# Spreading the PEER gates: one fp32 product per token, or two rounded (fp32r) products with the gate in two parts

## The reference, cut to what matters

```python
ids = jnp.take_along_axis(cand_i, best_pos, axis=-1)      # i * 128 + j
g = jax.nn.softmax(best_s, axis=-1)
...
ub = jnp.take(u_tab, idb, axis=0)
act = jax.nn.gelu(jnp.einsum('tkd,td->tk', ub, xb))
vb = jnp.take(v_tab, idb, axis=0)
return jnp.einsum('tk,tkd->td', gb * act, vb)
```

## Time and profile before

| | us |
|---|---|
| runs timed (3) | 2165.93 median, 2165.83 to 2167.42 |
| the profiled execution | 2171.05 |
| its span in the profile | 2169.3 |
| PE busy in it | 2108.0 (97%) |
| the stretch of the spreads | about 690 to 807 of the span |

### The profile page before, as it was taken

The page is one execution under the profiler, slowest core; times in us unless marked ns, Lnnn a source line. Parts: engine busy times, 40 slices in busy tenths (PEclk is TensorE's granted clock), DMA queues, the critical chain, the costliest instruction groups (busy, mean ns, idle before and its releaser), DMA issues.

```text
span 2169.3 us, 31600 instructions
## 1 busy us (share of the span) xinstructions
PE 2108.0 (97%) x12416; PEld 1897.5 (87%) x12416; DVE 1376.8 (63%) x1874; ACT 704.3 (32%) x745; POOL 4.8 (0%) x11
## 2 busy tenths in 40 slices
PE   7999998998999998999999999999999999999997
PEld 5888887887988998999999999989999999999785
DVE  6675575568788986556565655655555565654675
ACT  2014112005311344434334343433434334342432
POOL 0000000000000000000000000000000000000000
PEclk8999999999999999999999999999999999999999
DMA  9999595994443458555555555655555565555552
GB/s 390 421 419 362 197 365 236 380 421 172 171 155 116 180 216 319 206 179 209 188 218 193 195 207 176 219 189 207 204 183 207 186 222 189 200 206 177 196 193 78
DMA packets 98649, 496.12 MB, mean 229 GB/s; under 512 B 8256, under 2 KB 41312, under 8 KB 43040
## 3 DMA queue, kind: packets, MB, share of 16 engines
q1 hardware_dynamic: 83280, 373.81, 45.9%
q10 hardware_dynamic: 14112, 115.35, 14.0%
q0 software_dynamic: 1200, 6.16, 0.7%
HBM read 473.14 MB, written 22.15 MB: 228 GB/s over the span
## 4 chain that ended last, share of the span: by engine, by line
PE 89%; DMA 7%; DVE 3%; ACT 1%; issue 0%; ACTq 0%; DVEq 0%; SPq 0%; POOL 0%
PE ps L470 19%; PE ps L459 11%; PE ps L460 11%; PE ps L461 11%; PE ps L725 5%; PE ps L727 5%; PE ps L726 5%; PE ps L714 5%; PE ps L715 5%; PE ps L716 5%; DMA mod_first<-wmod 4%; PE ps L671 3%; DMA mod_ring<-wmod 1%; DVE mod_first L1112 1%; DMA wraw<-wst 1%; DVE rstd L1088 0%
## 5 line engine op out<-in xcount | busy, mean ns | idle before, releaser
L461 PE MATMUL ps<-h_hi,wlo 128*128 128x256 f32 x1952 | 553.3, 283 | 0.0
L459 PE MATMUL ps<-h_hi,whi 128*128 128x256 f32 x1728 | 490.0, 284 | 5.4 <-ACT act_u L954 5.4
L460 PE MATMUL ps<-h_lo,whi 128*128 128x256 f32 x1728 | 490.0, 284 | 0.0
L1411 DVE TENSOR_TENSOR yacc<-yacc,ps 128x512 f32<-128x512 f32 x256 | 176.1, 688 | 404.5 <-PE ps L727 404.5
L461 PEld LDWEIGHTS ps<-h_hi,wlo 128*128 128x128 f32 x1952 | 375.5, 192 | 0.0
L1377 DVE TENSOR_TENSOR vlo<-vraw,vhi 128x2048 fp32r<-128x2048 f32 x116 | 260.8, 2289 | 135.3 <-ACT vhi L1001 135.3
L459 PEld LDWEIGHTS ps<-h_hi,whi 128*128 128x128 f32 x1728 | 332.7, 193 | 7.6 <-issue 5.6
L460 PEld LDWEIGHTS ps<-h_lo,whi 128*128 128x128 f32 x1728 | 332.7, 193 | 2.0
L470 PE MATMUL ps<-hid,wraw 128*128 128x256 f32 x1344 | 296.6, 381 | 4.7 <-DVE hid L1258 4.7
L470 PEld LDWEIGHTS ps<-hid,wraw 128*128 128x128 f32 x1344 | 256.6, 191 | 40.7 <-issue 4.9
L1373 DVE TENSOR_TENSOR wlo<-wraw,whi 128x2048 fp32r<-128x2048 f32 x120 | 269.4, 2285 | 16.6 <-ACT whi L977 16.6
(11 more groups left out here) (239 smaller groups left out, 2336.1 us busy)
## 6 DMA issues: line engine op xcount, KB each, us to landing
vraw<-vtab SPq DMA_DIRECT2D x116, 1024.0 KB, 6.7
wraw<-wst SPq DMA_DIRECT2D x108, 1024.0 KB, 4.8
wraw<-wst ACTq DMA_DIRECT2D x94, 1024.0 KB, 7.1
mod_ring<-wmod SPq DMA_DIRECT2D x74, 1024.0 KB, 12.6
mod_first<-wmod SPq DMA_DIRECT2D x22, 1024.0 KB, 20.0
gates_dram<-gstage ACTq DMA_DIRECT2D x4, 4096.0 KB, 16.8
gring<-gates_dram SPq DMA_DIRECT2D x64, 256.0 KB, 5.1
wraw<-vtab SPq DMA_DIRECT2D x12, 1024.0 KB, 5.0
```

Source lines behind the costliest of these rows:

```text
L459: mm(dst, hi, src_hi, start=first, stop=False)
L460: mm(dst, hi, src_lo, start=False, stop=False)
L461: return mm(dst, lo, src_hi, start=False, stop=last)
```

## The change

Each token's single fp32 product becomes two fp32r products that accumulate in the same PSUM bank: `hot_a`.T @ `hot_b` with the gate's rounded upper part, and `hot_a`.T @ `hot_lo` with the remainder. ACT writes the rounded gates `gate_hi` (one more copy out of PSUM per half of the tokens). DVE computes once, for all 256 tokens, `gate_part` = (gate - gate_hi) / max(gate_hi, 1e-30) in four instructions. ACT makes `hot_lo` for each token by multiplying DVE's `hot_b` by the token's `gate_part` (one number per partition). PE waits for `hot_lo` in place of `hot_b`. In ACT's stream the remainder's one-hots of spread m+3 stand ahead of the copy of spread m, after three sets made up front; its loop is written out.

```diff
-        hot_a = at("hot_a", 173.5, [HOT_RING, GT, P])
-        hot_b = at("hot_b", 181.5, [HOT_RING, GT, P])
+        hot_a = at("hot_a", 173.5, [HOT_RING, GT, P], F32R)
+        hot_b = at("hot_b", 181.5, [HOT_RING, GT, P], F32R)
+        hot_lo = at("hot_lo", 149.5, [HOT_RING, GT, P], F32R)
+        gate_hi = at("gate_hi", 217.5, [T], F32R)
+        gate_part = at("gate_part", 218.5, [T])
@@ PE, spread
-                pe.wait_ge(s_hot, n + 1)
+                pe.wait_ge(s_hotlo, n + 1)
...
                 for t in range(GT):
-                    r = mm(ps_spread[r_][:, t, :], hot_a[:, r_, t, :], hot_b[:, r_, t, :], start=True, stop=True)
+                    mm(ps_spread[r_][:, t, :], hot_a[:, r_, t, :], hot_b[:, r_, t, :], start=True, stop=False)
+                    r = mm(ps_spread[r_][:, t, :], hot_a[:, r_, t, :], hot_lo[:, r_, t, :], start=False, stop=True)
@@ ACT
                 A(picks[:, :, tt * P:(tt + 1) * P], ps_spread[tt][:, 0:3], ACT.Copy).then_inc(s_pkr, 1)
+                A(gate_hi[:, tt * P:(tt + 1) * P], ps_spread[tt][:, 2], ACT.Copy).then_inc(s_ghi, 1)
+
+            def one_hots_lo(r_, n, first=False):
+                act.wait_ge(s_hot, n + 1)
+                if not first:
+                    act.wait_ge(s_gmm, n - (HOT_RING - 1))
+                for t in range(GT):
+                    r = A(hot_lo[:, r_, t, :], hot_b[:, r_, t, :].bitcast(F32), ACT.Copy,
+                          scale=gate_part[:, bass.ds(n * GT + t, 1)])
+                r.then_inc(s_hotlo, 1)
...
+            act.wait_ge(s_part, 1)
+            for n in range(HOT_RING - 1):
+                one_hots_lo(n, n, True)
...
-                    with act.Fori(0, per // HOT_RING) as i:
-                        for r_ in range(HOT_RING):
-                            act.wait_ge(s_gmm, i * HOT_RING + (m0 + r_ + 1))
-                            A(gstage[...], ps_spread[r_].rearrange("p t b -> p b t"), ACT.Copy).then_inc(s_gev, 1)
+                    for m in range(m0, m0 + per):
+                        if m + HOT_RING - 1 < SPREADS:
+                            one_hots_lo((m + HOT_RING - 1) % HOT_RING, m + HOT_RING - 1, m == 0)
+                        act.wait_ge(s_gmm, m + 1)
+                        A(gstage[...], ps_spread[m % HOT_RING].rearrange("p t b -> p b t"), ACT.Copy).then_inc(s_gev, 1)
                     early_gelu(b)
@@ DVE
             dve.wait_ge(s_pkr, 2)
+            dve.wait_ge(s_ghi, 2)
+            own.did(V.tensor_scalar(ms[:, 0, :], gate_hi[:].bitcast(F32), 1e-30, None, ALU.max)); own.settle()
+            own.did(V.reciprocal(ms[:, 1, :], ms[:, 0, :]))
+            own.did(V.tensor_tensor(gate_part[:], picks[:, 2, :], gate_hi[:].bitcast(F32), ALU.subtract)); own.settle()
+            V.tensor_tensor(gate_part[:], gate_part[:], ms[:, 1, :], ALU.mult).then_inc(s_part, 1)
...
-                    b, g = (picks[:, i, bass.ds(n * GT + t, 1)] for i in (1, 2))
+                    b, g = picks[:, 1, bass.ds(n * GT + t, 1)], gate_hi[:, bass.ds(n * GT + t, 1)].bitcast(F32)
                     r = V.tensor_scalar(hot_b[:, r_, t, :], iota, b, g, ALU.is_equal, ALU.mult)
```

More of the change, by code:

```diff
@@ L314, in hybrid_block @@
                                           sem("picks_transposed"), sem("picks_read"))
+        s_ghi, s_part, s_hotlo = sem("gate_hi"), sem("gate_lo_over_hi"), sem("one_hots_lo")
         s_hot, s_gmm, s_gev = sem("one_hots"), sem("gates_spread"), sem("gates_staged")
@@ L985, in _ @@
                     m0 = (b - FIRST) * per
-                    with act.Fori(0, per // HOT_RING) as i:
-                        for r_ in range(HOT_RING):
-                            act.wait_ge(s_gmm, i * HOT_RING + (m0 + r_ + 1))
-                            A(gstage[:, q % 2, :, bass.ds((i * HOT_RING + (m0 - q * 2 * per + r_)) * GT, GT)],
-                              ps_spread[r_].rearrange("p t b -> p b t"), ACT.Copy).then_inc(s_gev, 1)
+                    for m in range(m0, m0 + per):
+                        if m + HOT_RING - 1 < SPREADS:
+                            one_hots_lo((m + HOT_RING - 1) % HOT_RING, m + HOT_RING - 1, m == 0)
+                        act.wait_ge(s_gmm, m + 1)
+                        A(gstage[:, q % 2, :, bass.ds((m - q * 2 * per) * GT, GT)],
+                          ps_spread[m % HOT_RING].rearrange("p t b -> p b t"), ACT.Copy).then_inc(s_gev, 1)
                     early_gelu(b)
```

## The result

| | median us | range | runs |
|---|---|---|---|
| before | 2167.29 | 2165.83 to 2168.65 | 8 |
| after | 2172.48 | 2171.83 to 2176.13 | 8 |

The ratio is 1.0027, 95% interval 1.0016 to 1.0038: the change makes the kernel 5.2 us slower (3.5 to 8.2), where +6.6 was forecast. The profiled execution of after took 2171.83 us with a span of 2170.0. It isn't slower by 5 us than the profiled one of before (2171.05, 2169.3), because the parts that the change does not touch happened to be quicker, 1.8 us ahead of the spreads and 0.9 us behind them. So I compare the stage itself, from the start of the second turning of the picks to the first product of block 20: 806.78 - 689.36 = 117.42 us before, 808.40 - 687.54 = 120.86 us after, +3.4 us.

A forecast was written before the change was run, and what follows sets the result against it. PE bounds the kernel (97% busy), DVE nearly a second bound in the stage. Products 0, start +4.4, clock +0.7, stop +1.5 give +6.6 us: 2177.7 profiled, 2172.5 timed, say 2173; range 2162 to 2184.

The forecast's parts named there:

- the likeliest case: Whole kernel: products cost nothing, start, clock and stop add +6.6 us, 2173 us timed; chance 0.52.
- two of its terms: More half clock after the longer first wait, +0.7 us, and ACT's stop after chunk 18, +1.5 us.
- Products: PE's spreads: two fp32r products per token cost what one fp32 product did, change 0, ends -23 and +57 us.
- The choice of 0.111 us by the weight load: PE's spread records: the load of 128 columns limits a short fp32r product, 0.111 us each as before.
- The straight line through the products of 256 and 512 columns: PE's spread records: fp32r pace carried down to 128 columns gives 0.066 us, the lower end.
- rival (1): Spreads: fast products, 0.066 us a record, another engine sets the pace; 2168 us by ACT, 2163 by DVE; chance 0.26.
- Start: Before PE's first spread: `gate_hi` copy 0.25, four DVE instructions 2.9, ACT's first remainder 1.27; +4.4 us.
- Clock: Start of the spreads: PE's longer wait adds a little more half clock, +0.7 us, bounds 0 and 2.5.
- The stop at the third store: After chunk 18: ACT waits for the store and makes `whi`, PE waits for spread 59's remainders; +1.5 us, bounds 0 and 4.
- Behind the stage: After the spreads: PE's stop moves as a whole and absorbs nothing; its 5.44 us wait stays.
- ACT: Steady steps: four remainders, copy out and chunk-end share need 1.69 of 1.76 us, so ACT just fits.

The follow-up runs named there:

- two experiments with half operands: Changed kernel with 64 moving columns in both fp32r products, 2271.45 us; changed kernel with a stationary operand of 64 columns, 2168.88 us.
- start-only kernel: Kernel before with the four DVE instructions ahead of the first one-hots, their results unused: 2171.12 us, ratio 1.0018.
- the one with the fp32 product: Changed kernel with one fp32 product per token, `hot_b` alone; ACT still makes `hot_lo` and PE waits for it: 2172.90 us, ratio 1.0024.
- the two kernels with shared work: Changed kernel without the remainder, ACT multiplying three of four tokens' gates: 2148.94 us; the same with ACT's stop and first `whi` four spreads later: 2144.91 us.
- the repeat: Changed kernel unchanged, because an edit's condition held in all 64 spreads: 2172.25 us, ratio 1.0021.
- split start: Changed kernel with `gate_part` made in three pieces, the first of 16 tokens, DVE starting on the first half of the picks: 2170.12 us, ratio 1.0012.
- `whi` twice: Changed kernel with ACT making the first `whi`, after chunk 18, twice: 2173.96 us, ratio 1.0029.
- the stationary operand of 64: Changed kernel with `hot_a`'s first 64 columns as stationary operand in both fp32r products, all 128 moving columns kept: 2168.88 us, ratio 1.0003.
- six-copy kernel: Changed kernel with the remainder's copies of two of a set's four tokens each cut into two of 64 columns: 2194.03 us, ratio 1.0120.
- upper part only: Changed kernel without `hot_lo`, `gate_part` and its four DVE instructions, one fp32r product per token: 2156.87 us, ratio 0.9954.
- later `whi`: Shared-work kernel (no remainder, ACT multiplying three tokens' gates) with ACT's stop and first `whi` four spreads later: 2144.91 us, ratio 0.9891.

## Why the prediction was right, step by step

The forecast was +6.6 us and 2173, the likeliest case; 2172.48 and +5.2 were measured. Direction, place and mechanism were right: the products cost nothing, the start costs 4.3 us. That the forecast of 2172.5 was met to 0.1 us is luck: it stood on a median of before of 2165.93 from three runs, which is 2167.29 over eight, and two of its terms, worth 2.2 us together, were not found.

- **Products: 0 forecast, 0 found.** The choice of 0.111 us by the weight load was right, and the two experiments with half operands show the reason given to be the right one. The straight line through the products of 256 and 512 columns is not wrong, but it holds only while the product covers its load: with the load halved, 128 columns do run at 0.06. With the whole load the records stay about 0.11 us apart at 64 columns as at 128, so the fast products of rival (1) did not come. The rule of the Trainium skill (TensorE: Matmul & The Clock Gate, LDWEIGHTS), columns over 1.2 GHz, 107 ns for 128, agrees with the 0.11 us at full clock; at the half clock the measured 0.213 us is twice that, so here the load follows the granted clock, where the rule has one number. That a load hides behind one product only, which the prediction says in the same sentence, does not stand in that section; the traces of this case bear it out, since the records behind the four long ones of the chunk steps are 0.11 apart from the second on, as if no load had been made ahead.
- **Start: +4.4 forecast, +4.3 found** (7.22 - 2.88). DVE's four took 2.74 us for 2.9, ACT's first set 1.28 for 1.27, and the wait for `gate_hi` made DVE begin 0.24 us later for 0.25.
- **Clock: +0.7 forecast, -0.9 found.** From the first spread to block 20 the stage took 113.6 us after and 114.5 before. The half clock ended 4.2 us behind the first spread (699.0) where it had taken 6 us before, so less work fell into it. In the start-only kernel it is -1.3 us and in the one with the fp32 product -0.4. All of these are differences to one execution of before, and this length varies from one execution to the next: in the two kernels with shared work, which are the same up to the end of chunk 18, the first spread comes 2.64 us behind the picks in both, and the third starts 5.08 us behind the first in one and 3.56 in the other. So the term of +0.7 was not found, and the sign of what is in its place is not shown.
- **The stop at the third store: +1.5 forecast, 0 found.** This is the step that failed. ACT reached the stop when I said (796.6, t + 1.5 for t + 1.4, t being the start of spread 56 at 795.1), but the store had landed: at most 14.2 us after its issue, where the forecast carried over the 16.3 us of before. So ACT did not wait the 2.4 us, and `whi` alone, 1.8 us, is covered by the three sets of lead. With `whi` doubled the wait of PE appears, 0.97 us, which shows the mechanism as right; what was wrong is the duration of the DMA. This was no chance of one execution: the third store was there within 13.9 to 14.3 us, without a wait, in the repeat and in the kernels with one fp32 product, split start, `whi` twice and the stationary operand of 64 too, while start only, with the spacing of before, has 16.2 us. Why it lands sooner no run tests. One thing that differs is that ACT issues the load of weights 1.8 us ahead of the store in place of 0.5.
- **Behind the stage: nothing absorbed.** The remainder of the span is 1361.6 us after and 1362.5 before, and PE's stop there ends 23.6 us behind the start of the last spread for 23.8. It follows the last spread, as forecast. The kernels whose block 20 began late show the other side of it: what PE loses between the last spread and the stop is taken back.
- **ACT: 1.69 us a step forecast, 1.65 and the chunk ends found**, and the six-copy kernel places the bound where it was put.

The sum from the trace is 4.3 - 0.9 + 0 = 3.4 us in the stage. The timed +5.2 (3.5 to 8.2), and the repeat's +4.6 (2.6 to 6.5), are a little more. The repeat's interval has the 3.4 in it, and the half clock at the start, which moves by 1.5 us between executions of the same code, is one candidate. Where this last 1 to 2 us lies isn't shown, and I leave it open.

## What to carry to other kernels

The short products here are paced by the load of their stationary operand: two one-pass products of 128 by 128 (0.11 us each) cost what one fp32 product does. Of what would help, the runs show fewer products (10 us gained) and a narrower stationary operand (0.06 us a record), and the rows of 256 columns show wider ones (0.12 us for twice the columns). Before giving a neighbour engine work to relieve PE, add up its instructions per step, and price what now stands in front of the first product; here that start was the whole loss that the traces show. And in a stage where several engines are within 0.1 us of each other, look at each one's single long stops: a wait of 2.40 us cost another 3 us through the clock. A duration of a DMA is a weak thing to carry over to a kernel that issues its transfers at other times: here 16.3 us became at most 14.2.

## What the runs showed of the hardware that I had not expected

- PE with every record back to back, products of 64 moving columns behind loads of 128 between fp32 chunk steps, stayed at 1.2 GHz for over 200 us after it had fallen there in a wait, and cost 99 us against the changed kernel. The same records, started at 2.4 GHz, kept it for the rest of the stage (57 us, one execution).
- The load of 128 columns follows the granted clock: 0.11 us at 1.00 and 0.213 at 0.50, with products of 128 or 64 columns. With a load of 64 columns, 128 moving columns are 0.06 and 0.107 us apart.
- Waits of PE of 2.06 to 2.40 us in a busy stage were each followed by the half clock (six copies, load of 64, shared work), those of 0.97, 1.11 and 1.73 us were not (`whi` twice, split start, load of 64). The length of the wait alone doesn't decide it: at the end of the stage 1.58 us of idle time was followed by the half clock at once (upper part only), and so were 1.58 and 0.84 us, one step apart, 1.3 us later (later `whi`).
